# Expert rows picked and combined by one-hot products on chip instead of by gather, scatter and row store

## The reference

```python
t = rmsnorm(h, ffn_norm)                       # tokens x 1024
group, (expert, gate) = ...                    # best group of 8, then best 2 of its 8 experts
for each expert e with the rows xb routed to it:
    hdn = silu(xb @ w_gate[e]) * (xb @ w_up[e])    # 1024 -> 512
    y   = hdn @ w_down[e]                          # 512 -> 1024
out[token] += gate * y                         # each token gets two such rows
return rmsnorm(h + out, final_norm)[:, 16:]
```

## Time and profile before

| | us |
|---|---|
| median of 3 runs | 2644.92 |
| lowest, highest | 2644.49, 2645.21 |
| the profiled execution | 2641.53 |
| its span in the trace | 2639.7 |
| TensorE, VectorE, ScalarE, GpSimd busy | 2367.3, 893.0, 515.2, 177.0 |
| bytes read from and written to HBM | 566.66 MB, 20.97 MB |

### The profile page before, as it was taken

One profiled execution on the slowest core, in us unless ns is written; L12 is line 12 of the kernel. 1 busy time (PEld: TensorE's weight loads), 2 busy tenths in 40 slices (PEclk: granted clock), 3 DMA queues, 4 the chain that ended last, 5 costly groups with the idle time before them and its releaser, 6 DMA issues.

```text
span 2639.7 us, 27104 instructions
## 1 busy us (share of the span) xinstructions
PE 2367.3 (90%) x10571; PEld 1453.0 (55%) x10571; DVE 893.0 (34%) x1344; ACT 515.2 (20%) x865; POOL 177.0 (7%) x452
## 2 busy tenths in 40 slices
PE   8998999999899999999899997888888888888884
PEld 5887888566564888888545654333333333333331
DVE  4656653245463544442346424111111111111113
ACT  3111100255241211100311311111111111111112
POOL 0000000000000000000000001111111111111111
PEclk8998999999899999999999998989899999999997
DMA  7565521312102223222310036999999999999995
GB/s 259 188 217 182 188 88 44 96 49 52 61 0 64 64 86 118 64 88 67 122 37 32 1 134 269 411 418 415 408 414 404 413 404 411 401 415 414 401 403 234
DMA packets 160043, 563.48 MB, mean 213 GB/s; under 512 B 16604, under 2 KB 110060, under 8 KB 133728
## 3 DMA queue, kind: packets, MB, share of 16 engines
q1 hardware_dynamic: 149728, 554.10, 54.3%
q0 software_dynamic: 10240, 8.31, 1.0%
HBM read 566.66 MB, written 20.97 MB: 223 GB/s over the span
## 4 chain that ended last, share of the span: by engine, by line
PE 61%; DMA 28%; DVE 6%; ACT 2%; issue 2%; SPq 1%; ACTq 0%; POOL 0%; POOLq 0%; DVEq 0%
DMA slots<-in_expert_w_up 24%; PE ps L822 15%; PE ps L1350 11%; PE ps L861 10%; PE ps L908 4%; DMA slots<-in_w_mod 3%; PE ps L999 2%; PE ps L1267 2%; PE ps L1072 2%; PE ps L914 2%; PE ps L1070 1%; PE ps L1067 1%; PE ps L932 1%; PE ps L959 1%; DVE acc L1801 1%
## 5 line engine op out<-in xcount | busy, mean ns | idle before, releaser
L1350 PE MATMUL ps<-slots,xT 128*64 128x512 f32 x2048 | 516.7, 663 | 153.4 <-DMA slots<-in_expert_w_up 151.8
L1350 PEld LDWEIGHTS ps<-slots,xT 128*64 128x64 f32 x2048 | 157.1, 152 | 509.9 <-issue 304.0
L822 PE MATMUL ps<-hT,slots 128*128 128x256 f32 x1408 | 314.8, 382 | 7.2 <-ACT hT L1455 7.2
L2369 DVE COPY hT<-ps 128x256 f32<-128x256 f32 x64 | 27.1, 424 | 865.4 <-PE ps L1358 865.4
L822 PEld LDWEIGHTS ps<-hT,slots 128*128 128x128 f32 x1408 | 269.9, 192 | 45.5 <-issue 8.1
L822 PE MATMUL ps<-slots 128*128 128x256 f32 x1056 | 242.7, 387 | 6.6 <-ACT tmp L1470 4.6
L1369 PE MATMUL ps<-slots,hT 128*64 128x512 f32 x1024 | 233.8, 598 | 1.8 <-DVE hT L2369 1.8
L822 PEld LDWEIGHTS ps<-slots 128*128 128x128 f32 x1056 | 204.4, 195 | 36.2 <-ACT tmp L1470 4.9
L1711 ACT ACTIVATE xT<-ps 64x512 f32<-64x512 f32 x64 | 37.8, 590 | 589.3 <-PE ps L1350 589.3
L1369 PEld LDWEIGHTS ps<-slots,hT 128*64 128x64 f32 x1024 | 68.4, 136 | 115.4 <-issue 111.3
L861 PE MATMUL ps<-big,slots 128*128 128x256 f32 x528 | 116.6, 379 | 0.0
(11 more groups left out here) (381 smaller groups left out, 2757.3 us busy)
## 6 DMA issues: line engine op xcount, KB each, us to landing
slots<-in_expert_w_gate SPq DMA_DIRECT2D x64, 2048.0 KB, 17.1
slots<-in_expert_w_up SPq DMA_DIRECT2D x64, 2048.0 KB, 22.5
slots<-in_expert_w_down SPq DMA_DIRECT2D x64, 2048.0 KB, 23.2
slots<-in_w_mod SPq DMA_DIRECT2D x18, 2048.0 KB, 12.2
slots<-in_w_gate SPq DMA_DIRECT2D x22, 1024.0 KB, 5.4
slots<-in_w_up SPq DMA_DIRECT2D x22, 1024.0 KB, 8.0
slots<-in_w_down SPq DMA_DIRECT2D x8, 2816.0 KB, 10.2
slots<-in_w_in SPq DMA_DIRECT2D x24, 512.0 KB, 5.6
```

The costliest lines, as they stand in the source:

```text
L822: last = mm(bank[:, g], lhs[:, g, k], rhs[:, k], start=(first and g == 0 and k == 0), stop=(k == 3), skip_group_check=True)
L1350: last = mm(ps[g * CAP:(g + 1) * CAP, j, :], xsT[j][:, k, :], w[g][:, k, :], start=(k == 0), stop=(k == KC - 1))
L2369: v.tensor_copy(hid[j].rearrange("p c s -> p (c s)"), ps[:, 6 + j, 0:4 * CAP]).then_inc(s_hd, 1)
```

## The change

Blocks have 32 slots, and the loop runs over rounds ("quads") of four. One product set picks the rows of a whole round: TensorE multiplies the normed tokens in SBUF with a one-hot of 128 tokens by 128 slots, so that the result has slots as columns already (64 instructions a round), and ScalarE copies 128x1024 to `xsT`. Gate and up use four column groups of 32, two halves of 256 columns for gate and two for up; down uses four quarters of 256. The results of a round's four blocks stand in one tile `ys` of 128 slots, and eight products of 512 columns with a transposed one-hot that holds the gates give each token's share, which VectorE adds to `h2`; these are done in the next round behind gate and up of its second block, and for the last round at the end. VectorE makes the next round's one-hot and the gate one-hot in the loop; positions are lowered by 128 each round. Gone are: the store of `u2`, the index tables, all of GpSimd's gathers and scatters, and the reading back. SyncE's refill order is the same, two pairs to a round. The feed-forward's semaphore is renamed `s_dp`, so that L2155 waits for its own four exponentials.

```diff
-CAP = 64
+CAP = 32
+QUAD = 4
...
-            for t in range(NT):
-                sp.wait_ge(s_un, t + 1)
-                sp.dma_start(u_dram[t * P:(t + 1) * P, :], u2[:, t, :]).then_inc(s_ud, 16)
...
-            for j in range(2):
-                sp.wait_ge(s_scat[j], sp.snap(n_pairs * 16))
-            rows = y_dram.rearrange("(t p k) d -> t p k d", p=P, k=2)
-            for t in range(NT):
-                sp.dma_start(y2[t], rows[t]).then_inc(s_y2[t], 16)
...
+            def pick_rows(hot):
+                for k in range(KC):
+                    for t in range(NT):
+                        last = mm(flat[:, 2048 + k * P:2048 + (k + 1) * P], u2[:, t, :].rearrange("p (m k) -> p k m", k=KC)[:, k, :],
+                                  hot[:, t, :], start=(t == 0), stop=(t == NT - 1))
+                last.then_inc(s_xt, 1)
...
                     for g in range(2):
-                        last = mm(ps[g * CAP:(g + 1) * CAP, j, :], xsT[j][:, k, :], w[g][:, k, :], start=(k == 0), stop=(k == KC - 1))
+                        for h in range(2):
+                            at = 64 * g + 32 * h
+                            last = mm(ps[at:at + CAP, j, 0:256], xsT[:, k, i * CAP:(i + 1) * CAP], w[g][:, k, 256 * h:256 * (h + 1)],
+                                      start=(k == 0), stop=(k == KC - 1))
...
                 for c in range(4):
-                    for g in range(2):
-                        last = mm(ps[g * CAP:(g + 1) * CAP, 2 + j, :], hid[j][:, c, :], w[:, c, g * 512:(g + 1) * 512],
+                    for g in range(4):
+                        last = mm(ps[g * CAP:(g + 1) * CAP, 2 + j, 0:256], hid[j][:, c, :], w[:, c, g * 256:(g + 1) * 256],
                                   start=(c == 0), stop=(c == 3))
...
+            def combine(q):
+                pe.wait_ge(s_yc, value(q, 4, 4))
+                for n in range(2 * NT):
+                    if n >= 2:
+                        pe.wait_ge(s_sum, value(q, 8, n - 1))
+                    mm(ps[:, 4 + n % 2, :], gate_rows[:, n // 2, :], ys[:, n % 2 * 512:(n % 2 + 1) * 512], start=True,
+                       stop=True).then_inc(s_cmb, 1)
+
+            def quad(q, start=False, end=False):
+                gate_up(1, q)
+                if not start:
+                    combine(before(q))
+                turn_hidden(0)
+                down(0, q)
+                gate_up(2, q)
+                turn_hidden(1)
+                down(1, q)
+                if not start:
+                    pe.wait_ge(s_sum, value(q, 8, 0))
+                turn_gates(q)
+                gate_up(3, q)
+                turn_hidden(0)
+                down(2, q)
+                pe.wait_ge(s_gtc, value(q, 1, 1))
+                if not end:
+                    pe.wait_ge(s_oh, value(q, 1, 1))
+                    pick_rows(quad_hot)
+                    gate_up(0, behind(q))
...
+                turn_hidden(1)
+                down(3, q)
...
+            def rows_out(i, q):
+                act.wait_ge(s_my, value(q, 4, i + 3))
+                for g in range(4):
+                    last = av(ys[i * CAP:(i + 1) * CAP, g * 256:(g + 1) * 256], ps[g * CAP:(g + 1) * CAP, 2 + i % 2, 0:256], ACT.Copy)
                 last.then_inc(s_yc, 1)
...
+            def pick_quad():
+                for k in range(2):
+                    last = v.tensor_tensor(picked[k], pos[:, :, k].unsqueeze(2).to_broadcast([P, NT, P]),
+                                           const("iota").unsqueeze(1).to_broadcast([P, NT, P]), ALU.is_equal)
+                return last
...
+            def quad(q, start=False, end=False):
+                if not start:
+                    for t in range(NT):
+                        add_rows(before(q), t)
+                hidden_in(0, q)
+                hidden(1, q, 2)
+                for k in range(2):
+                    last = v.tensor_tensor(picked[k], picked[k], gates[:, :, k].unsqueeze(2).to_broadcast([P, NT, P]), ALU.mult)
+                step(last, q, 3)
+                v.tensor_tensor(gate_hot, picked[0], picked[1], ALU.add).then_inc(s_gh, 1)
+                hidden_in(1, q)
+                hidden(2, q, 4)
+                if not end:
+                    step(v.tensor_scalar(pos, pos, -float(P), None, ALU.add), q, 5)
+                    step(pick_quad(), q, 6)
+                    v.tensor_tensor(quad_hot, picked[0], picked[1], ALU.add).then_inc(s_oh, 1)
...
-                pool.indirect_dma_start(xs[j], None, u_dram, bass.IndirectOffsetOnAxis(tcol[j][:, :], 0),
...
-                pool.indirect_dma_start(y_dram, bass.IndirectOffsetOnAxis(acol[j][:, :], 0), ys[j], None,
```

More of the change, by code:

```diff
@@ L566, in build, with value, before, behind @@
         accs = [acc, acc_2[:, :]]
+        def value(q, each, more):
+            return q[0] * each + (q[1] * each + more)
+        def before(q):
+            return (q[0], q[1] - 1)
+        def behind(q):
+            return (q[0], q[1] + 1)
         block = ctx.enter_context(nc.Block())
@@ L1412, in _ @@
+            quad((0, 0), start=True)
+            with pe.Fori(0, n_more) as i:
+                quad((i, 1))
+            quad((n_more, 1), end=True)
+            combine((n_more, 1))
         @block.scalar
@@ new lines, in quad @@
+            def quad(q, end=False):
+                for i in range(QUAD):
+                    if i < QUAD - 1:
+                        gate_sigmoid(i + 1, q)
+                    elif not end:
+                        gate_sigmoid(0, behind(q))
+                    rows_out(i, q)
+                    if i == 1:
+                        gates_in(q)
+                    if i == 2 and not end:
+                        rows_in(behind(q))
+            rows_in((0, 0))
+            gate_sigmoid(0, (0, 0))
@@ new lines, in hidden_in, with add_rows @@
+            def hidden_in(i, q):
+                j = i % 2
+                dve.wait_ge(s_ta, value(q, 4, i + 1))
+                v.tensor_copy(hid[j].rearrange("p c s -> p (c s)"), ps[:, 6 + j, 0:4 * CAP]).then_inc(s_hd, 1)
+            def add_rows(q, t):
+                for g in range(2):
+                    n = 2 * t + g
+                    dve.wait_ge(s_cmb, value(q, 8, n + 1))
+                    v.tensor_tensor(h2[:, t, g * 512:(g + 1) * 512], ps[:, 4 + g, :], h2[:, t, g * 512:(g + 1) * 512],
+                                    ALU.add).then_inc(s_sum, 1)
@@ new lines, in quad @@
+            def quad(q, start=False, end=False):
+                if not start:
+                    for t in range(NT):
+                        add_rows(before(q), t)
[11 more added lines that the diff above has]
+                    v.tensor_tensor(quad_hot, picked[0], picked[1], ALU.add).then_inc(s_oh, 1)
+                hidden_in(2, q)
+                hidden(3, q, 5 if end else 7)
+                hidden_in(3, q)
+                if not end:
+                    hidden(0, behind(q), 1)
@@ L2381, in _ @@
+            hidden(0, (0, 0), 1)
+            quad((0, 0), start=True)
+            with dve.Fori(0, n_more) as i:
+                quad((i, 1))
+            quad((n_more, 1), end=True)
             steps[0] = 0
```

340 lines of the change are left out of this document (101 added, 239 removed).

## The result

| | before | after |
|---|---|---|
| median (lowest to highest), us | 2645.07 (2644.49 to 2647.34), 4 runs | 2573.01 (2570.95 to 2575.05), 4 runs |
| ratio to before | | 0.9726, 95% interval 0.9709 to 0.9743 |
| the profiled execution, its span | 2641.53, 2639.7 | 2571.93, 2570.0 |

What follows compares the result with a forecast made beforehand. The prediction took weight bytes and DMA engine time to bound the loop, with serial pieces at both ends. Start 4.3, stream 28.4 and end 20.5 sum to 53.2 us off 2644.9, giving 2592 us, range 2576 to 2622.

Steps and rivals of the forecast that it cites:

- The bound: Expert loop: bytes and DMA engine time count, TensorE waits 151.8 us for up weights; outside it, two serial pieces.
- The stream: First refill to last weight landing: removing indirect transfers saves 26.4 us and 2 more, 977.2 to 948.8 us, 411.7 GB/s.
- The two us that the prediction added for earlier slots: Near both ends of the stream: DMA engines falling short there should go as slots come free earlier, 2 us.
- The bounds of the stream: Weight stream: 977 us if weights alone flow no faster, 934 us at the best slice's 418 GB/s.
- Rival A: Stream: gathers were free in DMA time, so it stays at 965 to 977 us; time 2606 to 2620; chance 20%.
- Rival B: Stream: earlier freed slots let more transfers queue, 418 GB/s, 934 us; time 2577 us; chance 11%.
- Rival C: Loop: TensorE's round becomes the bound, 73 us against 61.2, deciding from 64.5; time about 2780 us; chance 6%.
- The start: One-hot to first freed slots: pick 9.3 us, faster gate and up; slots free at 1615.7 instead of 1620.0, 4.3 gained.
- TensorE's round: TensorE's work per four blocks: 40 us against 61.2 of DMA, pick 7.6, combine 6.8, four column groups fully overlapping.
- The end: Last weight landing to the kernel's end: about 22 us instead of 42.5, 20.5 gained, bounds 20 to 28.
- What would show it: Profile after: no software queue or POOL work, refill near 1616, 410 to 414 GB/s, TensorE 65% busy, last weights near 2564.
- the three signs named for being wrong: Loop: TensorE's weight waits vanish (Rival C), a round takes 62.5 us or more (Rival A), DMA share under 0.97.

Runs made afterwards that it cites:

- b_nogather: Kernel before with every gather index out of bounds, so no gathered row moves and scatters stay: 2599.55 us beside 2641.57 for the kernel before.
- x_gather: Kernel after plus 62 indirect gathers, each with 16 valid rows of 4 KB that nothing reads, one per block: 2613.88 us.
- x_gplain: Kernel after plus 62 plain transfers of 16 neighbouring 4 KB rows into partitions 0 to 15, without indices: 2610.55 us.
- b_early: Kernel before with half of the gate and up contraction left out, so weight slots come free some 3.5 us earlier per block: 2638.09 us beside 2642.72.
- x_contig_late: x_contig with the gate and up products done twice in every second block, so those slots come free later: 2565.84 us.
- x_late: Kernel after with every block's gate and up products done twice, so slots come free later: 2663.17 us.
- x_contig: Kernel after with `u2` stored permuted so the pick's weights are contiguous, router weights loaded in the same order: 2560.26 us, ratio 0.9685 to the kernel before.

## Why the prediction was wrong, point by point

**The bound**: right. The loop is a stream of weights in both kernels, TensorE waits for up weights (151.8 us before, 87.6 after), and the change acts through transfers removed and a shorter end.

**The stream, the step that failed.** The prediction put it so: "all indirect transfers. Their queue took 1.0% of 16 engines' span, 26.4 us". That share is the time of the queue's own packets; what they take from the weights was 56 us. The gathers are the mis-sized term: 13 us by their half of the share, 45 by b_nogather and 41 by x_gather. Scatters were sized about right (13 against 10 to 11). The two us that the prediction added for earlier slots are not to be found either: gathers and scatters make up the whole 56. The missing cost is that of where the rows land: 4 KB rows in 16 partitions held back the packets of the 2 MB weight loads, which go to all 128. The landing place itself was varied in the kernel after alone; a block of the kernel before packs its 9 to 26 rows into the first partitions in the same way, and its gathers lengthen the weights' packets as x_gather's do.

**The bounds of the stream** failed with it. The better end, 934 us, took the 418 GB/s of the best slice for what weights alone can reach; but all slices of the loop held gathers. 425 GB/s and 920.8 us are what it does without.

**Rival A** (gathers free in DMA time) is refuted by x_gather, x_gplain and b_nogather. **Rival B** came nearest in time, 2577, for a reason that does not hold: slots freed earlier brought no rate in b_early, and slots freed later took none in x_contig_late. That its time was near is luck. **Rival C** did not come, but was nearer than thought: TensorE begins to cost time from about 59 us a round at the faster stream and not from 61.2, and the round was 50 and not 40. x_late shows it: 14.6 us more a round, and 90 us lost.

**The start**: the sign was wrong, 4.3 gained forecast, 1.9 lost. The mis-sized term is "118 ns each" for the pick's instructions: the row matched in shape and type, not in stride, and they came 243 ns apart (15.53 us for 64). x_contig confirms cause and size: with contiguous weights the first pick takes 9.03 us, those in the loop 7.41 (116 ns each), and refill starts 6.3 us earlier, which would have made the forecast gain.

**TensorE's round**: products of four column groups, forecast 53 ns, took 57 (3.66 us for 64), so all four overlap, as the modulation row said (the profile has 46 weight loads in its 4.8 us, where the prediction counted 48; that gives 105 ns and changes nothing). A product of 256 columns alone would take 213 ns, half of the prediction's 427 for 512, so this is a factor of 3.7. The Trainium skill's page "TensorE: Matmul & The Clock Gate" (Measured speedup vs the span model) gives 3.07 for four row tiles; as an estimate from it the 64 products would have taken 4.5 us. The trace does not agree for these four column groups, and decides. The rest was the pick, 8 us more a round, and the combine, 7.7 instead of 6.8, which waits for VectorE's adds.

**The end**: 24.5 us against 22. The last up weights let gate and up start late, and at low clock: 6.44 us instead of 3.66, after 6.26 us of waiting. The last down (2548.74) then waits for these and the transposes instead of for its own weights, which landed at 2545.5, about when the down of the block before began (2545.32); the prediction had TensorE waiting for that landing. The combine's 16 products took from 2552.31 to 2563.24, since VectorE puts final rows between its adds; the last add ended 18.5 us behind the last landing, forecast 15.0, and what follows it took 6.0. The prediction's terms for that add up to 6.15, so that its end should read 21.2 and not "about 22".

**What would show it**: no software queue, no GpSimd work and DMA share 1.0 hold, and the long waits are for weights, though some 50 us of short ones for VectorE and ScalarE stand beside the 87.6. The rate (425, not 410 to 414), the first refill (1624.7, not 1616), the last weights (2545.5, not 2564) and TensorE's busy share in the loop (85%, not 65) were off, and pointed to the stream and to the pick at once. None of the three signs named for being wrong came: they covered rivals A and C and a DMA share that falls, and not a faster stream.

## What to carry to other kernels

A small transfer beside a saturated stream is not priced by its queue's share of DMA time, nor by its bytes alone: ask over how many and which partitions it lands, since here 64 KB cost 0.15 us over all 128, 0.3 us in every eighth and 0.6 us in the first 16. When a TensorE instruction is priced from a row of another line, shape and type are not enough; compare the stride at which its weights are read. The best rate seen in a stretch is no upper bound for the stream if every stretch holds the traffic that is to go.

The fastest version is x_contig: the change with `u2` stored in chunk order, 2560.3 us.

## What the runs showed of the hardware

- With weight loads saturating the DMA engines, 62 transfers of 16 rows of 4 KB (4.06 MB) cost 37.5 us into partitions 0 to 15, 19.4 into every eighth partition, and 9.0 as 512 bytes into each of 128. The weights' 16 KB packets grow with it, from 617 ns on average to 618 (128 partitions), 626 (every eighth) and 636 (0 to 15). Which resource behind the few partitions is the narrow one was not tried and stays open.
- An indirect gather all of whose 64 indices are out of bounds costs nothing that one run can show (2573.10 against 2573.01), and the form, indirect or plain, hardly counts (40.9 against 37.5).
- A 128x128 weight load of 32-bit floats takes 337 ns when its columns are 32 bytes apart and 192 ns when contiguous, and the products follow at its pace, 243 against 116 ns in the loop. The strided picks gain nothing from the clock: 15.53 us at the start, at a granted clock of 0.88, and 15.55 in the loop, at 1.00; the contiguous ones go from 9.03 (granted 0.82) to 7.41 (1.00). VectorE pays for the stored order: a 128x1024 write takes 2.01 us strided and 1.29 contiguous.
- The DMA share does not see this kind of loss: over 700 us of the loop it is 1.00 at 411 GB/s and 1.01 at 428.
